# HGRN units of a hybrid mixer: levels before decays, the next unit's preparation ahead of the state update, level 32 written in place

## The reference, cut to what matters

```python
def step(state, inp):                 # one chunk of tokens, one head
    qi, ki, vi, gi = inp
    b = jnp.cumsum(gi, axis=-2)       # gi is the log of the forget gate
    diff = b[:, :, :, None, :] - b[:, :, None, :, :]
    decay = jnp.exp(jnp.where(causal, diff, -jnp.inf))
    scores = jnp.einsum('bhtd,bhtsd,bhsd->bhts', qi, decay, ki)
    o = scores @ vi + (qi * exp(b)) @ state
    state = exp(b_last) * state + (ki * exp(b_last - b))^T @ vi
```

## Time and profile before

| | |
|---|---|
| median of 3 runs | 3621.81 us (3616.01 to 3624.19) |
| the profiled execution's own time | 3621.22 us |
| its span (first to last instruction) | 3619.4 us |
| instructions | 55175 |
| mean granted clock of TensorE | 0.976 |
| busy: PE, weight loads, DVE, ACT, POOL | 96%, 84%, 47%, 33%, 37% |
| unit stage of layer 0, 178 to 328 us | PE busy 130.8 of 150 us, granted clock 0.82 |
| unit stage of layer 1, 911 to 1061 us | PE busy 126.9 of 150 us, granted clock 0.85 |

### The profile page before, as it was taken

The page is one execution under the profiler, slowest core; times in us unless marked ns, Lnnn a source line. Parts: engine busy times, 40 slices in busy tenths (PEclk is TensorE's granted clock), DMA queues, the critical chain, the costliest instruction groups (busy, mean ns, idle before and its releaser), DMA issues.

```text
span 3619.4 us, 55175 instructions
## 1 busy us (share of the span) xinstructions
PE 3486.1 (96%) x20462; PEld 3050.4 (84%) x20462; DVE 1711.4 (47%) x2682; ACT 1180.3 (33%) x1908; POOL 1339.7 (37%) x530
## 2 busy tenths in 40 slices
PE   7998999989979999999999989999999989899999
PEld 6988999989979999888877768888888867788887
DVE  5465533544655435642446754245423544634242
ACT  2454322324553223321225542122222223422222
POOL 3312343432113434344432224444444434244443
PEclk9988999999889999999999999999999999999999
DMA  3211232322112323233332113333233323133333
GB/s 108 68 39 45 84 94 85 99 63 71 42 38 85 95 85 98 75 98 89 97 86 62 53 53 93 93 92 99 87 99 93 99 76 94 51 93 93 98 93 93
DMA packets 570036, 294.84 MB, mean 81 GB/s; under 512 B 10663, under 2 KB 568230, under 8 KB 569782
## 3 DMA queue, kind: packets, MB, share of 16 engines
q1 hardware_dynamic: 568724, 291.40, 27.6%
q0 software_dynamic: 768, 1.11, 0.1%
q10 hardware_dynamic: 418, 0.62, 0.0%
HBM read 291.00 MB, written 2.10 MB: 81 GB/s over the span
## 4 chain that ended last, share of the span: by engine, by line
PE 56%; issue 32%; POOL 8%; DVE 2%; ACT 1%; POOLq 0%; DMA 0%; SPq 0%; ACTq 0%; DVEq 0%
PE big L2031 46%; POOL wlow L708 8%; PE big L2432 3%; PE big L2072 2%; PE misc L2085 1%; PE misc L2201 1%; PE misc L2096 0%; PE misc L2481 0%; PE misc L2122 0%; PE big L2515 0%; ACT whigh L722 0%; DVE mix_psel L1603 0%; PE misc L2136 0%; DVE fresh L1538 0%; DVE mix_lev L1562 0%
## 5 line engine op out<-in xcount | busy, mean ns | idle before, releaser
L708 POOL TENSOR_TENSOR wlow<-raw,whigh 128x1024 fp32r<-128x1024 f32 (+1 forms) x508 | 1329.4, 2617 | 2248.0 <-ACT whigh L722 2248.0
L722 ACT CAST whigh<-raw 128x1024 fp32r<-128x1024 f32 (+1 forms) x508 | 563.8, 1110 | 2035.0 <-PE big L2031 1916.2
L2031 PE MATMUL big<-xhigh,whigh 128*128 128x512 f32 (+1 forms) x1744 | 551.3, 352 | 0.0
L2031 PE MATMUL big<-xlow,whigh 128*128 128x512 f32 (+1 forms) x1744 | 546.2, 349 | 0.0
L2031 PE MATMUL big<-xhigh,wlow 128*128 128x512 f32 (+1 forms) x1744 | 543.8, 348 | 0.0
L2031 PE MATMUL big<-ffn_x2l,whigh 128*128 128x264 f32 (+1 forms) x2016 | 539.9, 322 | 0.0
L2031 PE MATMUL big<-ffn_x2h,whigh 128*128 128x264 f32 (+1 forms) x2016 | 537.3, 321 | 2.1 <-DVE ffn_zg L1473 2.1
L2031 PE MATMUL big<-ffn_x2h,wlow 128*128 128x264 f32 (+1 forms) x2016 | 538.6, 321 | 0.0
L2031 PE MATMUL big<-ffn_hidl,whigh 128*128 128x264 f32 (+1 forms) x1408 | 421.6, 340 | 0.0
L2031 PE MATMUL big<-ffn_hidh,wlow 128*128 128x264 f32 (+1 forms) x1408 | 421.1, 340 | 0.0
L2031 PE MATMUL big<-ffn_hidh,whigh 128*128 128x264 f32 (+1 forms) x1408 | 419.2, 339 | 0.0
(11 more groups left out here) (402 smaller groups left out, 4092.0 us busy)
## 6 DMA issues: line engine op xcount, KB each, us to landing
raw<-in_ffn_w_gate_up SPq DMA_DIRECT2D x176, 512.0 KB, 3.8
raw<-in_ffn_w_down SPq DMA_DIRECT2D x96, 704.0 KB, 4.6
raw<-in_ffn_w_up SPq DMA_DIRECT2D x88, 512.0 KB, 3.8
raw<-in_w_in SPq DMA_DIRECT2D x52, 512.0 KB, 3.8
raw<-in_gmlp_w_in SPq DMA_DIRECT2D x32, 512.0 KB, 4.1
raw<-in_attn_w_in SPq DMA_DIRECT2D x24, 512.0 KB, 3.8
raw<-in_w_out SPq DMA_DIRECT2D x16, 512.0 KB, 3.9
raw<-in_gmlp_w_out SPq DMA_DIRECT2D x16, 512.0 KB, 3.9
```

The costliest lines, as they stand in the source:

```text
L708: eng.tensor_tensor(wlow[:, at0:at0 + n], raw[:, at0:at0 + n], whigh[:, at0:at0 + n].bitcast(F32), ALU.subtract).then_inc(slab_split, 1)
L722: eng.copy(whigh[:, at0:at0 + w], raw[:, at0:at0 + w]).then_inc(high_rounded, 1)
L2031: mm = eng.matmul(wide(big, slot, T)[:, c:c + n], w[:, (s * KC + k) * P:(s * KC + k + 1) * P], x[:, (x0 + k) * width + c:(x0 + k) * width ...
```

## The change

Three edits. The steps of a unit run in the order of `seq`: levels first, then steps 0 and 1; `scores` waits for the last level, and `to_tokens` gets a wait for step 1 (the line with `lev_ready.at(l, u, 1)`). The signals' places follow `steps`, which has the new order, and `scores` keeps naming the last level. `prep(u+2, 0)` stands ahead of `carry(u)` on DVE, and `exps(u+2, 0)` at the head of the unit on ACT, ahead of the slab's rounding; the scan no longer waits for the last exponent of unit u-2, and the wait for `headout` stands ahead of step 0's product. Level 32, like level 64, is written by PE straight into its place in the block of diagonal scores, by two products of 32 rows and 32 columns a head, and its COPY_PREDICATED goes; the mask gets two more blocks of ones.

```diff
--- before.py
+++ after.py
@@ -50,6 +50,7 @@
 
 CHUNKS = [(0, META)] + [(META + P * j, P) for j in range(SEQ // P)]
 LEVELS = [[8, 4, 2, 1], [64, 32, 16, 8, 4, 2, 1]]
+MERGED = LEVELS[1][2:]
 
 MIX_COLS = [(2048, 4), (2816, 2), (512, 4), (0, 4), (1024, 4), (2560, 2), (1536, 4), (3072, 2)]
 TILE_RQ, TILE_RK, TILE_RV, TILE_LX, TILE_HF, TILE_HQ, TILE_HI, TILE_RG, TILE_HG, TILE_LY = \
@@ -110,10 +111,12 @@
     squares = np.concatenate([sq[n] for n in SQUARES], 1).astype(f)
 
     masks = []
-    for (_, n), levels in zip((CHUNKS[0], CHUNKS[1]), (LEVELS[0], LEVELS[1][1:])):
+    for (_, n), levels in zip((CHUNKS[0], CHUNKS[1]), (LEVELS[0], MERGED)):
         parts = [np.eye(P)[:, :n]]
         if n == P:
             parts[0][0:64, 64:128] = 1.0
+            parts[0][0:32, 32:64] = 1.0
+            parts[0][64:96, 96:128] = 1.0
         for r in levels:
             q = np.arange(n).reshape(-1, 2, r)[:, 1, :].reshape(-1)
             first = np.arange(P)[:, None]
@@ -136,7 +139,7 @@
 
 
 LM0 = CHUNKS[0][1] + 8 * len(LEVELS[0])
-LM1 = P + 64 * (len(LEVELS[1]) - 1)
+LM1 = P + 64 * len(MERGED)
 
 
 
@@ -500,7 +503,8 @@
         L2 = range(2)
         CH = range(len(CHUNKS))
         UN = range(len(UNITS))
-        steps = [(l, u, j) for l in L2 for u in UN for j in range(2 + len(LEVELS[UNITS[u][0] > 0]))]
+        seq = [list(range(2, 2 + len(LEVELS[c > 0]))) + [0, 1] for c, _ in UNITS]
+        steps = [(l, u, j) for l in L2 for u in UN for j in seq[u]]
         fk_ready = Signal(sem("fk_ready"), [(l, i) for l in L2 for i in range(HH)])
         logf_ready = Signal(sem("logf_ready"), [(l,) for l in L2])
         decay_ready = Signal(sem("decay_ready"), [x for x in steps if x[2] >= 2])
@@ -515,7 +519,7 @@
         tok_ready = Signal(sem("tok_ready"), [(l, u, x) for l, u in every_unit for x in "vk"])
         scored = Signal(sem("scored"), every_unit)
         select_step = Signal(sem("select_step"), [(l, u, n) for l, u in every_unit
-                                                  for n in range(len(LEVELS[0]) if u == 0 else len(LEVELS[1]) - 1)])
+                                                  for n in range(len(LEVELS[0]) if u == 0 else len(MERGED))])
         masked = Signal(sem("masked"), every_unit)
         headout = Signal(sem("headout"), every_unit)
         upd_done = Signal(sem("upd_done"), inner_unit)
@@ -876,7 +880,7 @@
                     c, heads = UNITS[u]
                     w, nh = CHUNKS[c][1], len(heads)
                     b = bcum[:, 256 * (u % 2):256 * (u % 2) + nh * w]
-                    g0 = steps.index((l, u, 0))
+                    g0 = steps.index((l, u, 2))
                     if part == 0:
                         eng.wait_ge(scanned.sem, scanned.at(l, u))
                         if 0 < c < len(CHUNKS) - 1:
@@ -884,8 +888,8 @@
                             if c == 3:
                                 eng.wait_ge(state_ready.sem, state_ready.at(l, u - 4))
                             eng.activation(fend[:, f0:f0 + nh], b.rearrange("p (i t) -> p i t", i=nh)[:, :, w - 1], ACT.Exp)
-                    for j in range(0, CUT) if part == 0 else range(CUT, 2 + len(LEVELS[c > 0])):
-                        g = g0 + j
+                    for p in range(0, CUT) if part == 0 else range(CUT, len(seq[u])):
+                        g, j = g0 + p, seq[u][p]
                         e = fresh[:, T1 + (g % 2) * 256:T1 + (g % 2) * 256 + nh * w]
                         x = fresh[:, (g % 2) * 256:(g % 2) * 256 + nh * w]
                         if g >= 2:
@@ -1032,6 +1036,8 @@
                 tokens(0)
                 exps(1, 1)
                 for u in UN:
+                    if u + 2 <= LAST:
+                        exps(u + 2, 0)
                     if u < LAST:
                         if u == 2:
                             eng.wait_ge(lru_step.sem, lru_step.at(l, 1, 5))
@@ -1047,8 +1053,6 @@
                             eng.copy(c1(xhigh, 4 + j), src).then_inc(xhigh_ready, 1)
                         out_high(3)
                     out_copy(u)
-                    if u + 2 <= LAST:
-                        exps(u + 2, 0)
                     if u < LAST:
                         tokens(u + 1)
                     if u and u % 2 and u < LAST:
@@ -1518,7 +1522,6 @@
                     b = bcum[:, 256 * (u % 2):256 * (u % 2) + len(heads) * w]
                     if u >= 2:
                         eng.wait_ge(exp_ready.sem, exp_ready.at(l, u - 2, 1))
-                        eng.wait_ge(decay_ready.sem, decay_ready.at(l, u - 2, 1 + len(LEVELS[UNITS[u - 2][0] > 0])))
                     for n, i in enumerate(heads):
                         ins = eng.tensor_tensor_scan(b[:, n * w:(n + 1) * w], one[:, 0:w],
                                                      logf[:, i * T1 + tk:i * T1 + tk + w], 0.0, ALU.mult, ALU.add)
@@ -1565,21 +1568,16 @@
 
                 def prep(u, part):
 
-                    last = 1 + len(LEVELS[UNITS[u][0] > 0])
                     if part == 0:
                         scan(u)
                         exponent(u, 2)
-                        if u >= 2:
+                        exponent(u, 3)
+                    for p in range(0, CUT) if part == 0 else range(CUT, len(seq[u])):
+                        if p + 4 < len(seq[u]):
+                            exponent(u, seq[u][p + 2])
+                        if seq[u][p] == 0 and u >= 2:
                             eng.wait_ge(headout.sem, headout.at(l, u - 2))
-                        for j in range(CUT):
-                            if j:
-                                exponent(u, j + 2)
-                            product(u, j)
-                    else:
-                        for j in range(CUT, last + 1):
-                            if j + 2 <= last:
-                                exponent(u, j + 2)
-                            product(u, j)
+                        product(u, seq[u][p])
 
                 def select(u):
 
@@ -1595,7 +1593,7 @@
                         eng.wait_ge(headout.sem, headout.at(l, u - 2))
                     eng.tensor_tensor(dst, src[:, :, 0:w], mask[:, 0:w].unsqueeze(1).to_broadcast([w, nh, w]),
                                       ALU.mult).then_inc(select_step.sem, 1)
-                    levels = [r for r in LEVELS[c > 0] if r != 64]
+                    levels = LEVELS[0] if c == 0 else MERGED
                     for k, r in enumerate(levels):
                         eng.wait_ge(select_step.sem, select_step.at(l, u, k))
                         col = w + k * (w // 2)
@@ -1777,6 +1775,8 @@
                     select(u)
                     if u < LAST:
                         prep(u + 1, 1)
+                    if u + 2 <= LAST:
+                        prep(u + 2, 0)
                     if UNITS[u][0] < len(CHUNKS) - 1:
                         carry(u)
                     if u == LAST:
@@ -1791,8 +1791,6 @@
                         out_low(3)
                     if u % 2 == 0:
                         out_root(u // 2)
-                    if u + 2 <= LAST:
-                        prep(u + 2, 0)
                     if u == 6:
                         out_gate(0)
                         out_gate(1)
@@ -2195,8 +2193,10 @@
                         for k, r in enumerate(levels):
                             l0 = 7 * s1 + k * 256 + n * w
                             m = lev[:, l0:l0 + w]
-                            if r == 64:
-                                mm = eng.matmul(bank[0:64, 64:128], m[:, 0:64], m[:, 64:128], start=True, stop=True)
+                            if c and r not in MERGED:
+                                for s in range(0, w, 2 * r):
+                                    mm = eng.matmul(bank[s:s + r, s + r:s + 2 * r], m[:, s:s + r], m[:, s + r:s + 2 * r],
+                                                    start=True, stop=True)
                                 continue
                             mm = eng.matmul(bank[:, col:col + w // 2], m,
                                             m.rearrange("p (g two r) -> p g two r", two=2, r=r)[:, :, 1, :],
@@ -2214,6 +2214,7 @@
                     else:
                         eng.wait_ge(tok_ready.sem, tok_ready.at(l, u - 1, "k"))
                         eng.wait_ge(state_ready.sem, state_ready.at(l, min(u - 1, LAST - 2)))
+                    eng.wait_ge(lev_ready.sem, lev_ready.at(l, u, 1))
                     for name, at0 in (("v", 0), ("k", 3 * BANK if u == 0 else 256)):
                         for n, i in enumerate(heads):
                             src = v[:, i * T1 + tk:i * T1 + tk + w] if name == "v" else kdec[:, s1 + n * w:s1 + (n + 1) * w]
```

## The result

| | before | after |
|---|---|---|
| median | 3619.84 us (4 runs) | 3583.41 us (4 runs, 3582.23 to 3589.20) |
| ratio | | 0.9905, 95% interval 0.9893 to 0.9917 |
| the profiled execution's time, its span | 3621.2, 3619.4 us | 3583.7, 3581.9 us |
| mean granted clock | 0.976 | 0.985 |
| unit stages of both layers | 297.3 us | 261.6 us |

The account below looks back on a forecast made before the run. TensorE works 96% of the span, so only its waits and granted clock can be won. Waits -8.2, middle drops -13.8, remaining gaps +4, small matmuls +2: total -16.0, giving 3605 us, range 3592 to 3615.

Parts of the forecast that it names:

- Waits: TensorE's waits in both unit stages: 27 us in all after the change against 35.2 before, -8.2 us.
- Small matmuls, +2: Level 32 on TensorE: four 32-column matmuls replace two of 64 a head of a chunk, +2 us over 32.
- by the columns, 24 of 56 of the way: Price of a 32-column matmul, placed between 0.043 us (8 columns) and 0.129 (64): 0.080 us each.
- Clock, middle of the stage, -13.8: Half-clock drops of about 10 us at 235, 266 and 969 lose their gaps: 3 x 4.6 = -13.8 us.
- Clock, the gaps that remain, +4: Four TensorE gaps of 0.9 and 1.35 us remain; one in three draws a drop of 3 us net: +4.
- the drops after unit 0 and the two of 24 us stay: Clock drops after unit 0 (10 us) and at each stage's end (24 us) stay as they were: no gain.
- More goes: Rival: VectorE wins 0.3 us per pair, four waits and their drops go, end drops shrink: 3592 us, chance 0.08.
- The order does nothing: Rival: VectorE's busy time and the stage-end chain hardly change, won time becomes waits there: 3619 us, chance 0.08.
- The slower rival: Rival: carry's state comes late, to_tokens waits in each of 12 inner units: +14 us, 3635 us, chance 0.07.

Follow-up runs that it names:

- e3: The kernel before with level 32 written in place alone; median 3604.36 us, ratio 0.9968.
- e9: The kernel before with the new order of the steps and level 32 in place, without the move of prep(u+2, 0); 3603.75 us, ratio 0.9968.
- e10: The kernel before with prep(u+2, 0) and exps(u+2, 0) moved ahead and level 32 in place, without the new order; 3600.32 us, ratio 0.9956.
- e7: The kernel after with carry(6) put ahead of prep(8, 0) on VectorE; 3595.64 us, ratio 0.9938 to the kernel before.
- e13: The kernel after with eighteen added GpSimd memsets that TensorE waits for ahead of scores(8); 3600.09 us, ratio 0.9946 to the kernel before.
- e8: The kernel after with ScalarE's two SiLUs, out_high(0), out_high(1) and the VectorE block needing them one unit later; 3583.58 us, ratio 0.9906 to before.
- e15: The kernel after with the SiLUs' block one unit later, carry(0) ahead of prep(2, 0), select(8) ahead of out_low(2) and out_gate(3); 3580.42 us, 0.9895 to before.
- e1: The kernel before with the new order of the steps alone; median 3616.67 us, ratio 0.9995.

## Why the prediction was right or wrong

**Where the time is.** Right: only the unit stages changed, and both idle time and clock moved.

**Waits.** Right. In us of layer 0, each forecast and then measured: `scores(1)` 1.6, 2.08; `to_tokens(4)` 0.9, 0.59; `to_tokens(6)` 1.35, 1.35; `to_tokens(7)` 2.4, 2.69; `apply(7)` 1.4, 0.58; `scores(8)` 0.9, 0.58; `apply(8)` 4.9, 5.00; sum 13.5, 12.9 (layer 1 measured 12.7). In both stages the idle time fell by 9.4 us, forecast 8.2. The place of each new wait was foretold too.

**Small matmuls, +2.** Wrong sign. Four instructions of 32 columns take 257.11 - 256.92 = 0.19 us, 0.048 each, where two of 64 columns in the same run take 2 x (258.28 - 257.11) / 10 = 0.23. That is -0.04 a head, -1.4 us over 32; by the work of the stages at full clock it is -1.9 (four kernels without the part, 217.1 on average, against 215.2 in e3, e9, e10 and after). The step "by the columns, 24 of 56 of the way" failed: it gave 0.080 us an instruction, and 0.048 was measured. The number of columns alone doesn't set the price here. In after the four start at 256.924, 256.930, 256.976 and 256.983, so the two instructions of a product start 0.006 us apart. The bounds of the forecast were coarse as well, since 0.34 / 8 and 1.55 / 12 count the end of the last matmul in: in a stream of their own kind the matmuls of 8 columns start 0.025 us apart and those of 64 mostly 0.112. By the Trainium skill, "TensorE: Matmul & The Clock Gate", section on the back-to-back issue gap, matmuls of 1 to 64 columns take about the same time; this case's trace disagrees, 0.048 us at 32 columns against 0.117 at 64 (level 64's own two, 64 columns on 64 columns of weights, start 0.107 us apart).

**Clock, middle of the stage, -13.8.** Right: the drops at 235, 266 and 969 are gone, in both layers the clock is 1.0 up to unit 7. But the reading behind it, that two gaps in a row draw a drop, is not a rule. The kernel before has the same pair of gaps as ahead of 266 once more, in layer 1, and there the clock stays at 1.0:

```profile
996.29 0.49 PE L2237 MATMUL misc<-mix_vtok,mix_psel 128*128 128x128 f32 x2 [0.46 <-DVE mix_psel L1603]
...
999.50 0.49 PE L2192 MATMUL misc<-mix_q,mix_kk 128*128 128x128 f32 x2 [1.61 <-DVE mix_lev L1562]
```

```profile
996.00:1008.00 12.00, 10.10 (x81) 9.54 (x82) 9.34 (x34) 8.96 (x31) 2.35 (x1) 1.00 0.16 46
```

In e3 the gap of 1.61 us is in all four places too; two drew a drop of 6.8 us and two none. So length and place of one gap don't settle whether a drop comes; the comparisons of places above rest on four gaps each and on the medians of whole kernels.

**Clock, the gaps that remain, +4.** The size was near, the reason not. The charge was laid on four gaps of 0.9 and 1.35 us, which drew nothing; the two of 2.7 us in `to_tokens(7)`, charged with nothing, drew 3.4 us each, 2 x 3.4 x 0.45 = 3.1 us. That the sizes agree is luck.

**Clock, "the drops after unit 0 and the two of 24 us stay", 0.** This is the step that failed. The two at the end held 17.5 and 14.5 us of PE work (the two windows of before above) and hold 3.3 and 4.7 now: 0.45 x (32.0 - 8.0) = 10.8 us. Those after unit 0 went from 10.2 and 10.2 to 6.8 and 10.3, 1.5 us. The prediction gives no reason for this nothing. It had itself forecast that the gaps at which these drops begin, ahead of `apply(7)` and `scores(8)`, would shrink to 1.4 and 0.9 us, and only the wait ahead of `apply(8)` stays. The experiments show what made them long: idle time ahead of `apply(7)` and `scores(8)` (4.24 us at 296.90 in the earlier trace rows). e7 and e13 bring such a gap back and with it drops of 17 to 24 us. In after `apply(8)` still waits 5.0 us, but the output projection's dense matmuls follow 1.9 us behind it and the drop ends after 3.4 us in layer 0; in layer 1 it lasts 6.9, of which 2.1 lie in the wait. In e8 and e15 neither gap is there, and yet a drop of 13.7 us comes with the gap ahead of `out_turn(3)`, small products too. So the gap need not stand ahead of `apply(7)` or `scores(8)`.

**The sum.** By the three-way split the forecast was waits -8.2, clock -9.8, work +2; measured -9.4, -23.4, -2.9. Of the 19.7 us missed, the clock has 13.6, the work 4.9 and the waits 1.2. The clock's share is placed: 10.8 at the two ends, 1.5 behind unit 0 and 0.9 on the gaps that remain (3.1 for 4) make 13.2. Of the work, the small matmuls have some 3.4 to 3.9; the rest isn't placed. One execution of after differs from another by up to 7 us, so the last us of such a sum shouldn't be pressed.

**Rivals.** "More goes" (3592, chance 0.08) had the right direction at the end, with half a drop a layer; it gave too little there, and the four waits that it took away stayed. "The order does nothing" is true of the order alone (e1). The slower rival didn't come: `to_tokens` waits in three inner units a layer, not in six.

**What stays open.** Place is shown to matter, but no rule here foretells each drop, and whether the work ahead of a gap or the work behind it counts was not tested apart. In e1 a gap of 2.53 us ahead of an `apply` drew no drop in layer 0 and 3.4 us in layer 1; in e9 one of 2.27 at the same place drew 10.2 us in both. After unit 0 a drop of 6.8 to 13.7 us comes in every kernel, whether `scores(1)` waits 0.88 or 2.28 us. Level 32 alone gained 12 us with unchanged idle time because drops went (x 0.45, 8.2 of the 9.4 us in its stages); why they went, and why it gained next to nothing on top of the move, stays open.
